# A decoder step on one core: the sample state as moving operand, block outer products, the convolution spread over the inversion, and small transfers moved off ScalarE's queue

## The reference, cut to what matters

```python
h = rmsnorm(x, g_mix); u = h @ w_in                     # 1024 -> 3080
conv_out = silu(layernorm(depthwise31(glu(u)) + b_dw))  # 512 channels
q, k, v, g, beta = gdn_inputs(u, ...)                   # 4 heads x 128, short conv of 4 taps
# prompt: chunked delta rule, a triangular inverse per chunk of tokens and head
# sample: one step per sequence, for every (sequence b, head h):
s = s * exp(g)                                          # s is 128 x 128
v = (v - s.T @ k) * beta
s = s + outer(k, v);  o = s.T @ q
x = x + concat(conv_out, rmsnorm(o) * silu(z)) @ w_out
x = x + cross_attn(rmsnorm(x), memory keys/values)      # sample: own cached 256 rows each
x = x + moe(rmsnorm(x))                                 # 32 experts, top 4, 12.6 MB of weights each
y = rmsnorm(x)
```

## Time and profile before

| | |
|---|---|
| timed runs | 1380.12, 1380.72, 1385.28 us, median 1380.72 |
| profiled execution, its own time | 1386.9 us |
| span of that execution | 1385.2 us |
| busy, TensorE / VectorE / ScalarE / GpSimd | 95% / 33% / 16% / 2% |
| moved by the transfer engines | 470.00 MB, mean 339 GB/s |

### The profile page before, as it was taken

How to read it: one execution, slowest core, us unless ns; L and a number is a source line. 1 busy time by engine, 2 the same in 40 slices (tenths; PEclk the granted TensorE clock), 3 DMA queues, 4 the chain that set the end, 5 groups by cost and what they waited for, 6 DMA issues and landing times.

```text
span 1385.2 us, 17643 instructions
## 1 busy us (share of the span) xinstructions
PE 1311.4 (95%) x6645; PEld 630.3 (45%) x6645; DVE 463.5 (33%) x1319; ACT 220.2 (16%) x447; POOL 34.5 (2%) x71
## 2 busy tenths in 40 slices
PE   4998988999788999999999999999999999999996
PEld 2877786468564333333333333333333333333332
DVE  2664437823633223322232222322233222332224
ACT  2241021232212001010110101110011100111002
POOL 3000012001000000000000000000000000000000
PEclk9999987999998999999999999999999999999998
DMA  9231052568792999999999999999999999999992
GB/s 310 69 122 62 0 193 93 169 235 324 299 409 110 377 428 427 429 427 429 429 428 429 427 429 428 429 429 428 429 427 430 428 429 429 428 429 428 429 430 90
DMA packets 56652, 470.00 MB, mean 339 GB/s; under 512 B 6852, under 2 KB 7077, under 8 KB 32029
## 3 DMA queue, kind: packets, MB, share of 16 engines
q1 hardware_dynamic: 50256, 457.23, 79.6%
q0 software_dynamic: 3264, 11.40, 2.3%
q10 hardware_dynamic: 3101, 0.94, 0.4%
HBM read 463.84 MB, written 6.29 MB: 339 GB/s over the span
## 4 chain that ended last, share of the span: by engine, by line
PE 86%; DMA 5%; DVE 5%; ACT 2%; ACTq 1%; issue 1%; DVEq 0%; POOL 0%; SPq 0%; POOLq 0%
PE bank L950 51%; PE bank L531 11%; PE bank L996 5%; DMA ring<-in_w_gu 5%; PE bank L765 4%; PE bank L963 3%; PE bank L982 2%; PE bank L976 1%; ACTq L1067 1%; DVE ring L1709 1%; PE bank L670 1%; PE bank L590 1%; PE bank L738 1%; PE bank L678 1%; PE bank L843 1%
## 5 line engine op out<-in xcount | busy, mean ns | idle before, releaser
L950 PE MATMUL bank<-ring,region_p 128*64 128x512 f32 x2304 | 504.7, 595 | 1.7 <-DMA ring<-in_w_gu 1.0
L950 PEld LDWEIGHTS bank<-ring,region_p 128*64 128x64 f32 x2304 | 163.4, 137 | 327.2 <-issue 323.4
L1864 DVE TENSOR_SCALAR region_p<-bank 128x512 f32<-128x512 f32 x32 | 22.1, 692 | 615.5 <-PE bank L982 615.5
L950 PE MATMUL bank<-region_m,region_p 128*64 128x512 f32 x768 | 169.5, 593 | 0.5 <-DMA region_m<-in_w_gu 0.5
L531 PE MATMUL bank<-hT,ring 128*128 128x264 f32 x512 | 121.1, 396 | 0.0
L1841 DVE TENSOR_TENSOR xT<-xT,bank 128x264 f32<-128x264 f32 x264 | 95.5, 424 | 60.6 <-PE bank L996 60.6
L531 PEld LDWEIGHTS bank<-hT,ring 128*128 128x128 f32 x512 | 99.3, 196 | 17.5 <-issue 0.4
L950 PEld LDWEIGHTS bank<-region_m,region_p 128*64 128x64 f32 x768 | 54.4, 137 | 108.6 <-issue 107.3
L950 PE MATMUL bank<-region_p 128*64 128x512 f32 (+1 forms) x396 | 99.7, 622 | 3.8 <-DVE region_p L1826 3.8
L1335 ACT COPY region_p<-bank 128x264 f32<-128x264 f32 x33 | 12.5, 378 | 475.1 <-PE bank L976 475.1
L996 PE MATMUL bank<-region_p 64*128 64x264 f32 x528 | 81.0, 415 | 0.5 <-ACT region_p L1335 0.5
(11 more groups left out here) (363 smaller groups left out, 923.2 us busy)
## 6 DMA issues: line engine op xcount, KB each, us to landing
ring<-in_w_gu SPq DMA_DIRECT2D x96, 2048.0 KB, 20.6
ring<-in_w_dn SPq DMA_DIRECT2D x48, 2048.0 KB, 24.7
region_m<-in_w_gu SPq DMA_DIRECT2D x32, 2048.0 KB, 22.1
region_m<-in_w_dn SPq DMA_DIRECT2D x16, 2048.0 KB, 26.1
ring<-in_w_in SPq DMA_DIRECT2D x6, 2048.0 KB, 11.9
ring<-in_cache_mem_k SPq DMA_DIRECT2D x6, 1024.0 KB, 14.3
ring<-in_cache_mem_v SPq DMA_DIRECT2D x6, 1024.0 KB, 9.4
ring<-in_w_mk SPq DMA_DIRECT2D x2, 2048.0 KB, 7.8
```

The lines of the kernel that those rows point to most:

```text
L950: ins = pe.matmul(bank[n][u * SLOTS:(u + 1) * SLOTS, :], lhs, rhs, start=start, stop=stop)
L1864: dve.tensor_scalar(xg, bank[0][:, :], 7.0, None, ALU.min).then_inc(sem("glu_clipped"), 1)
```

## The change

Five edits are made together.

1. **Queues at the start.** Ten of ScalarE's eighteen loads are issued by SyncE behind the first weight block, three more (`conv_rows`, `wr`, `br_bc`) by ScalarE after its first reads of banks; SyncE no longer waits for the parameters before block 1. The gain of the first norm gets a job of its own (`gmix`); `x_t` 0 to 7 move between the `qkv` jobs, read out by ScalarE alone.
2. **Filler matmuls.** `stay_busy` issues matmuls of a matrix of ones, 512 columns each, with no use of the result: 3 before `gmix`, 4 before `xn_t` 0, 1 before `s_attn_t`, 3 before `xo` 0, and 4 after the routing jobs.
3. **Inversion.** `z` 2 goes ahead of it, the four `glu_b`/`glu_a` pairs are the fillers of levels 1 to 4, the token transposes and `qk` of level 5, `z` 3 of level 6. The convolution steps stand behind the second half's `inv_t` and `inv_d` in tens and sixes.
4. **Sample work.** `s_read` becomes two jobs of 4 matmuls with q and k of four sequences (32 columns) as stationary operand, each in a 32-column part of the array, and the state as moving operand of 512 columns. ScalarE copies the two products, and `s_rd` picks the wanted rows by 8 matmuls. `s_krow` and `s_vrow` transpose k and v, VectorE spreads v into block form (`v_blocks`), and each of the 8 `s_outer` jobs is one matmul of 32 rows and 512 columns, an outer product for four heads. VectorE adds the decayed state in one instruction; GpSimd's multiplication is gone.
5. **Order after it.** `s_outer` stands behind `mk` 1; 20 convolution steps stand ahead of the state's update on VectorE.

```diff
-    jobs = [("param", 0)] + [("xn_t", c) for c in range(8)] + [("x_t", c) for c in range(8)]
-    jobs += [("param", 1), ("qkv", 0), ("short_hist",), ("ab",), ("qkv", 1), ("ab_t",)]
...
+    jobs = [("gmix",)] + [("xn_t", c) for c in range(8)]
+    jobs += [("qkv", 0), ("param", 0), ("param", 1), ("short_hist",), ("ab",), ("qkv", 1), ("ab_t",), ("x_t", 0)]
...
-    fill = [[("z", 2)], [("v_tok", 0), ("v_tok", 1)], [("z", 3)], [("k_tok", 0), ("k_tok", 1), ("qk", 0), ("qk", 1)]]
-    fill += [[(n, i)] for i in range(4) for n in ("glu_b", "glu_a")]
+    fill = [[(n, i)] for i in range(4) for n in ("glu_b", "glu_a")]
+    fill += [[("v_tok", 0), ("v_tok", 1), ("k_tok", 0), ("k_tok", 1)], [("qk", 0), ("qk", 1)], [("z", 3)]]
...
-    jobs += [("s_decay",), ("s_kq",), ("s_read",)] + [("mem_t", c) for c in range(8)]
+    jobs += [("s_decay",), ("s_kq",), ("s_krow",), ("s_read", 0), ("s_read", 1)] + [("mem_t", c) for c in range(8)]
+    jobs += [("s_rd",), ("mk", 0), ("s_vrow",), ("mk", 1)]
     jobs += [("s_outer", g) for g in range(sample_groups)]
-    jobs += [("mk", t) for t in range(4)]
+    jobs += [("mk", 2), ("mk", 3)]
...
+            BUSY = {("gmix",): 3, ("xn_t", 0): 4, ("s_attn_t",): 1, ("xo", 0): 3}
+
+            def stay_busy(dst, n):
+                for _ in range(n):
+                    pe.matmul(dst[:, :].rearrange("p (r n) -> p r n", r=4), ones[:, :],
+                              ones[:, :].unsqueeze(1).to_broadcast([P, 4, P]), start=True, stop=True)
...
-                    for b in range(TS):
+                    pe.wait_ge(sem("k_pad"), 1)
+                    for j in range(4):
+                        b = 4 * m + j
+                        ins = pe.matmul(ps(key)[32 * j:32 * j + 32, :], qk_s[:, m, :, :].rearrange("p f j -> p (f j)"),
+                                        s_state[:, b * H:(b + 1) * H, :].rearrange("p c n -> p (c n)"), start=True,
+                                        stop=True)
...
-                    for j in range(GROUP):
-                        c = key[1] * GROUP + j
-                        ins = pe.matmul(ps(key)[:, j * P:(j + 1) * P], s_v[:, c:c + 1].to_broadcast([P, P]),
-                                        ident[:, :], start=True, stop=True)
-                    filled(ins, key)
+                    m, j = divmod(key[1], 4)
+                    open_bank(pe, key)
+                    wait_drained(pe, "s_krow")
+                    wait_drained(pe, "s_vrow")
+                    filled(pe.matmul(ps(key)[:, :], k_row[32 * j:32 * j + 32, :],
+                                     v_blocks[32 * j:32 * j + 32, 4 * m:4 * m + 4, :].rearrange("p r n -> p (r n)"),
+                                     start=True, stop=True), key)
...
+            wait_drained(pe, "h_tok", 0)
+            stay_busy(ps(("h_tok", 0)), 4)
...
-                if key[0] == "inv_t" and key[1] >= 4 or key[0] == "inv_d" and key[1] >= 5:
-                    conv_some(4)
...
+                    if c == 1 and lv >= 2:
+                        conv_some(10)
...
+                    if c == 1 and 3 <= lv < LEVELS - 1:
+                        conv_some(6)
...
+            conv_some(8)
...
+            conv_some(12)
```

More of the change, by code:

```diff
@@ L731, in _ @@
                     filled(pe.matmul(ps(key)[:, 0:BH], ones[:, :], s_kq[:, :], start=True, stop=True), key)
+                elif kind in ("s_krow", "s_vrow"):
+                    open_bank(pe, key)
+                    pe.wait_ge(sem("k_pad" if kind == "s_krow" else "v_pad"), 1)
+                    src = k_pad if kind == "s_krow" else v_pad
+                    filled(pe.transpose(ps(key)[:, 0:P], src.rearrange("p j r -> p (j r)"), ident[:, :]), key)
                 elif kind == "s_read":
+                    m = key[1]
@@ L736, in _ @@
+                    filled(ins, key)
+                elif kind == "s_rd":
+                    open_bank(pe, key)
+                    pe.wait_ge(sem("pick"), 1)
+                    rd = ps(key)[:, 0:2 * BH].rearrange("p (b h k) -> p b h k", b=TS, h=H)
+                    for m in range(2):
+                        wait_drained(pe, "s_read", m)
                         for h in range(H):
-                            c = b * H + h
-                            ins = pe.matmul(ps(key)[:, 2 * c:2 * c + 2], s_state[:, c, :],
-                                            qkv[:, h:h + H + 1:H, TP + b], start=True, stop=True)
+                            ins = pe.matmul(rd[:, 4 * m:4 * m + 4, h, :], s_prod[m][:, h * P:(h + 1) * P],
+                                            pick[:, :, :, h], start=True, stop=True)
@@ L1127, in _ @@
                 drained(act.mul(hT[:, c, :], ps(("xn_t", c))[:, 0:T], pcol("mix", c)), ("xn_t", c))
-            for c in range(1, 8, 2):
-                wait_filled(act, "x_t", c)
-                drained(act.copy(xT[:, c, :], ps(("x_t", c))[:, 0:T]), ("x_t", c))
+            load(conv_rows[0:120, :, :], st_conf[0].rearrange("b j c -> (b j) c").rearrange("(a p) c -> p a c", a=2),
+                 "conv_rows_in")
+            load(wr, w_router[0].rearrange("(k p) n -> p k n", p=P), "wr_in")
+            load(br_bc, b_router[0:1, :].to_broadcast([P, E]), "wr_in")
             def softplus_parts():
@@ L1188, in _ @@
             z_copy(1)
+            z_copy(2)
+            wait_drained(act, "param", 0)
             def glu_gate(i):
@@ L1222, in _ @@
             drained(act.copy(s_beta, ps(("s_decay",))[:, BH:2 * BH]), ("s_decay",))
+            wait_filled(act, "s_krow")
+            drained(act.copy(k_row, ps(("s_krow",))[:, 0:P]), ("s_krow",))
+            for m in range(2):
+                wait_filled(act, "s_read", m)
+                drained(act.copy(s_prod[m], ps(("s_read", m))[:, :]), ("s_read", m))
             for c in range(8):
@@ L1236, in _ @@
                         ("mk", j))
-            wait_drained(act, "s_read")
+            wait_drained(act, "s_rd")
             for h in range(H):
@@ L1435, in _ @@
                         ("xn_t", c))
-            for c in range(0, 8, 2):
-                wait_filled(dve, "x_t", c)
-                drained(dve.tensor_copy(xT[:, c, :], ps(("x_t", c))[:, 0:T]), ("x_t", c))
+            param(0)
             param(1)
```

121 lines of the change are left out of this document (74 added, 47 removed).

## The result

The changed kernel took 1348.22 us, the median of four timed runs (1345.48 to 1349.69). Beside it the kernel before took 1383.0 us (1380.12 to 1385.41, four runs). The ratio is 0.975, with a 95% interval of 0.972 to 0.978: 35 us less. The prediction said 1341, with a range of 1330 to 1354; its likeliest case, 1335 to 1346, is missed by 2 us.

The account below looks back on a forecast made before the run. The expert weights stream without pause at 428 GB/s, so time saved in the 445 us before them counts one for one. Five terms sum to 39.6: 1386.9 becomes 1347.3, less 6.2 is 1341, range 1330 to 1354.

Parts of the forecast that it names:

- likeliest case: Whole kernel: all five terms near their value, 35 to 46 us saved, 1335 to 1346 us; chance 50%.
- Start and projections (16.4): Start to last `qkv`: ends at 70.4 instead of 86.8 us, 16.4 saved, bounds 9.8 to 18.5.
- The step that failed is the last one: Final sum: 1347.3 us lowered by the 6.2 the profiled execution lay above the median, giving 1341.1.
- the second rival: Matmuls of ones don't hold the clock at start, `xo` and experts: 23.5 us saved, 1357, half of it 1349; 16%.
- Inversion (7.7): Up to `w_neg`: levels 1 to 4 at 12.24 us, VectorE bounding level 5; `w_neg` 7.7 us earlier, bounds 2 to 14.
- Sample work (8.5): From `w_neg` to `ln_mean`: 79.0 us against 87.5, state landing at 17.9; 8.5 saved, bounds 1 to 17.
- The rival that the state comes on time: Sample work: TensorE doesn't idle and the clock stays high, 5 and 3 us more saved, 1333; 16% for 1324 to 1335.
- `xo` (2.9): Head of `xo`: three matmuls of ones in the wait for VectorE hold the clock, 2.9 us saved.
- entry to the experts (4.1): First gather and first weights: four matmuls of ones in the routing wait hold the clock, 4.1 us saved.

Follow-up runs that it names:

- e6_start_only: The kernel before with only the start's edit (queues, `gmix`, order of `x_t`), without matmuls of ones: 1373.38 us, ratio 0.994.
- e2: The change with SyncE loading the sample state and memory rows ahead of weight blocks 7 and 8: 1344.47 us, ratio 0.973.
- e4: The change with both the state loaded ahead of the weight blocks and the convolution steps moved out of level 5: 1337.86 us, ratio 0.967.
- e7: The change with the sample work of before (old `s_read`, `s_outer` ahead of `mk`, decay on GpSimd): 1367.58 us, ratio 0.990.
- e12: The change with the inversion's fillers and convolution steps as before, 32 steps there instead of 66: 1358.90 us, ratio 0.982.
- e5: e4 with four more matmuls of ones, ahead of `xn_t` 4, `mem_t` 0 (two) and the position job: 1336.68 us, ratio 0.966.
- e10_no_start_ones: e4 without the seven matmuls of ones at the start, those at `xo` and after the routing kept: 1338.56 us, ratio 0.969.
- e9_matmul_turn: e4 with plain matmuls with the identity in place of the transposes of `xn_t` and `h_tok`: 1337.34 us, ratio 0.969.
- e3_conv_moved: The change with the convolution steps taken out of level 5, into levels 2 to 4 and behind the last `inv_t`: 1340.46 us, ratio 0.968.
- e1_no_ones: The change without its 15 matmuls of ones: 1356.35 us, ratio 0.981.

## Why the prediction was right, and where it was off

The forecast was faster, by five terms that sum to 39.6 us. The profiled executions differ by 41.8, and the median is 7.1 us above the forecast. The medians differ by 34.8, so 4.8 of the 7.1 are time that was not saved. The other 2.3 are the starting point: 1380.72 was the median of three runs, and with a fourth it is 1383.0; the other groups gave 1382.9 to 1383.8.

**Start and projections (16.4).** In the first pair it measured 16.6, with errors that cancel: the last x came at 8.13 and not 6.50, which put `xn_t` at 10.95 and not 10.2, and `qkv` 0 took 3.76 and not 4.7. In the second pair it measured 10.0, and this is where the forecast of the median was off. The step that failed is the last one, "that execution lay 6.2 above the median of the runs, 1380.7, so 1341.1 as the new median". It carries the 6.2 over to the changed kernel. But the second profile of before, 4.5 us shorter, is 3.75 us shorter in the start (3.0 because ScalarE's loads stalled it less, 0.7 in `qkv` 0) and 2.2 us in the inversion. The start's stall is what the change removes, so that excess stands once in the term (20.98) and once more in the shift. And the shift was itself too large: against 1383.0 the profiled execution lay 3.9 above, not 6.2. With the second profile's 83.06 as the start the term is 12.7 and the sum 35.9; the second pair gave 35.5. `e6_start_only` agrees with the smaller start, 10.2 us by the medians.
The other part of the loss is the clock. Eight profiled executions started with the same matmuls (the two of the change, `e2` to `e4`, `e7`, `e12`, and `e5` with one more); `qkv` 0 took 3.76 us in two and 5.3 to 6.1 in six. So 3.76 was the exception, and `e10_no_start_ones` shows that the ones bring next to nothing there. That is the second rival, true for the start only. The Trainium skill, TensorE: Matmul & The Clock Gate, Part 4, says that transposes do not count as busy for the clock. `e9_matmul_turn` is in line with it (1.00 with plain matmuls), as are six of the eight profiles. Two of eight with transposes also kept the clock, so one profile of `e9` does not prove it.

**Inversion (7.7).** Right: 7.3 and 5.6. Levels 1 to 4 took 12.24 each. VectorE came last in level 5; the copy that level 6 waits for ended 13.8 us after level 4's last transpose was filled (153.08 - 139.24, the level's start less 0.45 as in the forecast), where 14.2 was forecast, and the fallen clock cost 2.7 in `inv_x` and `z` 3 (3.76 + 4.48 against 2.02 + 3.56) where 2 was counted. `e3_conv_moved` took the steps away and got 6.8 us back.

**Sample work (8.5).** Measured 10.8 and 11.0. The state landed 19.3 us behind `w_neg` (17.9 forecast), `s_read` took 3.64 (3.5), `mk` 0 began at 27.7 (28.1). That last agreement is in part luck: the state came 1.4 us later than forecast, and `mem_t` (2.92 for 3.7) and `s_rd` (1.69 for 2.9) were shorter by 2.0. The 2.7 us for the clock in `mk` 0 were too much: it took 6.97, since the clock was back by 190. The outer products took 2.00 us (1.8), in this row of TensorE's timeline:

```profile
205.82 2.00 PE L801 MATMUL bank<-region_p,rn 32*128 32x512 f32 x16
```

So the row parts overlap 3.4 times (6.9/2.0). The Trainium skill, TensorE: Matmul & The Clock Gate, Part 3, gives 3.07 for such parts, by which 2.2 was the estimate. VectorE's convolution was done 2.0 us ahead of `ln_mean` (1.5 forecast). `e2_state_first` shows that the late landing cost 5.3 us of this term, as the steps had it (block 7, block 8 and the state in one queue). The rival that the state comes on time fell; made to happen, it brought 5.3 us behind `w_neg`, where that rival had counted 8.

**`xo` (2.9) and entry to the experts (4.1).** 2.6 and 3.0, 4.9 and 5.4. `e1_no_ones` gives 2.7 and 4.8 us back when the ones are gone.

**What the parts are worth together.** By the medians the start alone saves 10.2 us. Left out of the change, the ones cost 8.1, the sample's part 20.4, the inversion's 10.7. These sum to 49 where the whole saves 35, and the stages show why: the inversion's edit is worth much more with the sample's edit than without it. With the old sample work the kernel with start, ones and the new inversion saves 16.0 (`e7`); 10.2 and 8.1 are the start's and the ones', so the inversion's edit brings about -2 there, an estimate. The stages of `e7` agree: it gains 5 to 7 us up to `w_neg` and loses 10.1 up to `ln_mean` (97.5 against 87.4), where the state now lands late and its 20.07 us stand in the chain. With the new sample work the edit brings 10.7, of which up to 3.5 are the entry's, by its one profile. There it also takes 34 convolution steps off VectorE, which in `e12` stand ahead of `ln_mean`.

**Open.** Why the clock stands at one level in one case and at the other in the next. At the start one and the same kernel showed both. What goes with it is how long the first three matmuls of ones took, in the change's first profile and in its second:

```profile
1.07 4.82 PE L598 MATMUL bank<-ones 128*128 128x512 f32 x6 [1.07 <-POOL ones L451]
...
1.08 5.49 PE L598 MATMUL bank<-ones 128*128 128x512 f32 x6 [1.08 <-POOL ones L451]
```

In the two executions with `qkv` 0 at 3.76 they took 4.82 and 4.74 us, in the six others 5.30 to 5.49. So the clock had risen earlier in the two, before the transposes began; what made it rise earlier is not shown. `e9_matmul_turn`, with 5.22 nearer to the six, kept the clock all the same, which speaks for its theory. At the entry the level went with the kernel: the first weights took 13.95 in the change, twice, and in `e3` and `e7`, but 15.6 in the six other kernels with ones there (`e2`, `e4`, `e5`, `e9`, `e10`, `e12`), in one profile each. In the six the state had landed 9.8 to 11.2 us after its issue, in the others 19.5 to 20.1, 200 us earlier; but the matmuls just ahead of the ones took the same to 0.01 us in both groups (`e5` and `e9` apart). Whether the early state or chance decides it is not shown. More matmuls of ones did not settle it (`e5`). It matters for `e2`: against the change's second profile it gains 5.1 us from `w_neg` to `ln_mean` and 1.1 from there to `xo`, and loses 3.2 between `xo` and the end, which is why less than 5.3 came out.

The best version of those run is the change with the state first and the convolution steps moved: 1337.86 us, 10 us less than the change and 46 less than before. `e5`, `e9` and `e10` lie within 1.3 us of it and can't be told from it.

## What to carry to other kernels

An excess of the profiled execution over the median belongs to some stage: before shifting a sum by it, find the stage, and if the change removes what varies there, don't count it twice; a second profile of the kernel before shows it, and three runs are few for a median that the forecast starts from. When an edit speeds up the stage ahead of a transfer, the transfer's queue is next: the loads that a faster stage releases early go ahead of the one that the next stage waits for, so issue the urgent one first. A filler matmul paid here where TensorE waits ahead of long work at full clock (`xo`, the gather) and brought next to nothing ahead of a train of transposes. Edits that take the same engine off a path should be tried together and apart, since the value of one can be nothing without the other.

## What the runs showed of the hardware that was not expected

- **VectorE was held while GpSimd worked.** While GpSimd multiplied the state by the decay in two operations (7.17 us), two of VectorE's small operations took 3.5 us each, and the second ended at 212.5, when GpSimd did; the same two take 0.2 us in the change, where GpSimd no longer does this. All four profiled executions with that multiplication show it (the two of before, `e6`, `e7`), none without it does. No run takes the multiplication alone away. The timeline of the kernel before, in its second profile:

```profile
205.32 7.17 POOL L482 TENSOR_TENSOR ring<-ring,small 128x2048 f32<-128x2048 f32 x2 [6.56 <-PE bank L738]
205.47 3.53 DVE L1654 TENSOR_TENSOR small<-region_p,small 128x32 f32<-128x32 f32 x1
```

VectorE's timeline of the change:

```profile
192.28 0.22 DVE L1720 TENSOR_TENSOR small<-region_p,small 128x32 f32<-128x32 f32 x1
```

Those 7 us stood in the chain of before, ahead of the outer products, and are a part of what the sample work gained that the prediction did not name; it took the stretch as a whole from the earlier trace rows.

- **An f32 transpose was cheaper than the matmul with the identity.** At 2.4 GHz the 24 transposes of `xn_t` took 4.54 us and the 24 matmuls 7.81.
- **The start of the kernel before varies with the stalls of ScalarE's loads**: `xn_t` began at 20.98 in one execution and at 17.96 in the other, with the same queue.
